# Short convolution with tokens on partitions, its shifts by DMA, and the first two output units interleaved, in a two-layer hybrid decoder trunk

## The reference

```
u = x * (1.0 + sc1) + sh1
proj = u @ w_in[l]                                   # 2048 -> 6144
q, k, v, gate_b, gate_c, h_in = split(proj)          # 1024 columns each
attn = dilated_mixture(rotary(q), rotary(k), v)      # 8 heads of 128
conv = gate_b * causal_short_conv(gate_c * h_in, conv_w[l])   # three taps: t-2, t-1, t
mixed = group_rms_norm(concat([attn, conv]), mix_norm_g[l])   # over groups of 128 columns
x = layer_norm(alpha * x + (1.0 + g1) * (mixed @ w_out[l]), ln1_g[l], ln1_b[l])
```

## Time and profile before

| | |
|---|---|
| timed runs | 2361.34, 2363.52, 2365.28 us |
| profiled execution, own time | 2359.68 us |
| its span | 2358.0 us |
| PE busy | 2275.1 us |
| DVE busy | 1727.1 us |
| ACT busy | 1101.9 us |
| moved by DMA | 623.15 MB, 264 GB/s in the mean |

### The profile page before, as it was taken

One profiled execution on the slowest core, in us unless ns is written; L12 is line 12 of the kernel. 1 busy time (PEld: TensorE's weight loads), 2 busy tenths in 40 slices (PEclk: granted clock), 3 DMA queues, 4 the chain that ended last, 5 costly groups with the idle time before them and its releaser, 6 DMA issues.

```text
span 2358.0 us, 30332 instructions
## 1 busy us (share of the span) xinstructions
PE 2275.1 (96%) x10480; PEld 1884.4 (80%) x10480; DVE 1727.1 (73%) x1929; ACT 1101.9 (47%) x1392; POOL 227.3 (10%) x400
## 2 busy tenths in 40 slices
PE   3899999999999999999999999999999999999997
PEld 2777887878888888888878888877888888888886
DVE  6889888877777777668878878777666555555566
ACT  1345543366445445435454554435553543543542
POOL 3311111110001001001010001101000000000000
PEclk9899999999999999999999999999999999999999
DMA  9987888967888888888966888886677776666574
GB/s 379 409 318 274 311 320 313 341 216 255 286 297 287 285 285 300 288 276 289 323 228 196 271 265 288 285 273 224 194 238 239 226 231 212 215 205 195 170 232 133
DMA packets 174734, 623.15 MB, mean 264 GB/s; under 512 B 19728, under 2 KB 20496, under 8 KB 174096
## 3 DMA queue, kind: packets, MB, share of 16 engines
q1 hardware_dynamic: 114128, 407.50, 50.6%
q0 software_dynamic: 55296, 201.35, 25.6%
q10 hardware_dynamic: 5184, 12.59, 1.7%
HBM read 619.27 MB, written 2.10 MB: 264 GB/s over the span
## 4 chain that ended last, share of the span: by engine, by line
PE 87%; DVE 6%; DMA 3%; issue 2%; ACT 1%; ACTq 0%; POOL 0%; DVEq 0%; SPq 0%; POOLq 0%
PE bank L1323 27%; PE bank L1325 26%; PE bank L1324 26%; DMA Z<-w_mod_dram 2%; DVE mod_acc L808 2%; PE bank L1428 2%; DVE w_lo L793 1%; PE bank L1337 1%; PE bank L1403 1%; PE bank L1339 1%; PE bank L1338 1%; ACT w_hi L480 1%; PE bank L1412 1%; DMA raw<-w_out_dram 0%; PE bank L1572 0%
## 5 line engine op out<-in xcount | busy, mean ns | idle before, releaser
L480 ACT ACTIVATE w_hi<-raw 128x1024 fp32r<-128x1024 f32 x764 | 807.6, 1059 | 1135.7 <-PE bank L1325 1015.2
L793 DVE TENSOR_TENSOR w_lo<-raw,w_hi 128x1024 fp32r<-128x1024 f32 x764 | 932.9, 1224 | 550.7 <-ACT w_hi L480 548.9
L1323 PE MATMUL bank<-w_hi,u_hi 128*128 128x512 f32 x1744 | 698.0, 400 | 0.3 <-DVE u_lo L851 0.3
L1325 PE MATMUL bank<-w_lo,u_hi 128*128 128x512 f32 x1744 | 684.1, 392 | 0.0
L1324 PE MATMUL bank<-w_hi,u_lo 128*128 128x512 f32 x1744 | 684.0, 392 | 0.0
L1323 PE MATMUL bank<-w_hi,m_hi 128*128 128x512 f32 x1200 | 470.9, 392 | 4.5 <-DVE m_lo L851 2.6
L1324 PE MATMUL bank<-w_hi,m_lo 128*128 128x512 f32 x1200 | 468.4, 390 | 0.0
L1325 PE MATMUL bank<-w_lo,m_hi 128*128 128x512 f32 x1200 | 468.3, 390 | 0.0
L1325 PEld LDWEIGHTS bank<-w_lo,u_hi 128*128 128x128 f32 x1744 | 330.5, 189 | 70.7
L1323 PEld LDWEIGHTS bank<-w_hi,u_hi 128*128 128x128 f32 x1744 | 330.9, 190 | 68.8 <-issue 1.4
L1324 PEld LDWEIGHTS bank<-w_hi,u_lo 128*128 128x128 f32 x1744 | 331.0, 190 | 68.0 <-issue 1.4
(11 more groups left out here) (144 smaller groups left out, 1138.3 us busy)
## 6 DMA issues: line engine op xcount, KB each, us to landing
raw<-w_ff_dram SPq DMA_DIRECT2D x512, 512.0 KB, 4.2
mod_raw<-w_mod_dram POOLq DMA_DIRECT2D x320, 512.0 KB, 5.6
raw<-w_in_dram SPq DMA_DIRECT2D x192, 512.0 KB, 5.3
Z<-w_mod_dram POOLq DMA_DIRECT2D x64, 512.0 KB, 11.0
raw<-w_out_dram SPq DMA_DIRECT2D x64, 512.0 KB, 6.1
gate<-b_rows_dram ACTq DMA_DIRECT2D x4, 1024.0 KB, 5.0
Z<-ln_g_dram ACTq DMA_DIRECT2D x16, 256.0 KB, 6.5
Z<-ln_b_dram ACTq DMA_DIRECT2D x16, 256.0 KB, 7.3
```

The costliest lines, as they stand in the source:

```text
L480: nc.scalar.activation(weights(w_hi, u_hi, unit, j), raw[:, j % RAW, :], ACT.Copy).then_inc(hi_ready, 1)
L793: nc.vector.tensor_tensor(weights(w_lo, u_lo, unit, j), raw[:, j % RAW, :], weights(w_hi, u_hi, unit, j).bitcast(F32), ALU.subtract).then_ ...
L1323: nc.tensor.matmul(o, hi[:, k, tok], wh, start=(k == 0), stop=False)
L1325: ins = nc.tensor.matmul(o, hi[:, k, tok], wl, start=False, stop=(k == KC - 1))
```

## The change

The convolution keeps tokens on partitions. A shift by one or two tokens is then a shift by partitions, done by DMA from A into `back[1]` (the tile B) and `back[2]` (the tile V): for a shift of one, 112 and 15 partitions and one row from the first half of the tokens to the second; for a shift of two, 126 partitions and two rows. ACT issues these five transfers at group 64 (88), after three loads that put the taps as rows on all partitions at 61 (72). DVE multiplies and adds in tiles of 128 x 1024 at groups 66 and 68 (90 and 92). B is no longer copied or transposed: DVE multiplies it in from its accumulator behind unit 8 + 3g. ACT sums squares with its accumulator at 72 (96), DVE scales by the root at 74 (98), and PE transposes once, at 77 (101), where ACT puts the gain in.

Units 12 and 13 are interleaved: j = 0 to 5 of unit 12, 0 to 5 of unit 13, then 6 and 7 of each; w_out is laid out in memory in that order. Their residuals run behind groups 109 and 111.

```diff
-Z_AT = [66, 90]
-B_AT = [72, 96]
-SSQ_AT = [74, 98]
-R_AT = [76, 100]
+ROWS_AT = [61, 72]
+SHIFT_AT = [64, 88]
+CONV_AT = [66, 90]
+SHIFT_ROWS = {1: ((0, 112), (112, 127)), 2: ((0, 126),)}
+SUM_AT = [72, 96]
+VAR_AT = [73, 97]
+ROOT_AT = [74, 98]
+Y_AT = [77, 101]
+def out_order(i):
+    if i < 12:
+        return i // 6, i % 6
+    return (i - 12) // 2, 6 + i % 2
+OUT_DONE = [max(i for i in range(2 * GROUPS) if out_order(i)[0] == u) for u in range(2)]
 # ACT
+            def load_taps(layer, g):
+                for tap in range(3):
+                    row = 3 * layer + tap
+                    act.dma_start(taps[:, tap, :], conv_rows[row:row + 1, g * NCOL:(g + 1) * NCOL]
+                                  .to_broadcast([P, NCOL])).then_inc(taps_in, 16)
+                        if p == SHIFT_AT[g]:
+                            act.wait_ge(acc_read[h_unit % 2], h_unit // 2 + 1)
+                            for d in (1, 2):
+                                for lo, hi in SHIFT_ROWS[d]:
+                                    act.dma_start(back[d][lo + d:hi + d, :, :], A[lo:hi, :, :]).then_inc(shift_in, 16)
+                                act.dma_start(back[d][0:d, 1, :], A[P - d:P, 0, :]).then_inc(shift_in, 16)
+                        if p == SUM_AT[g]:
+                            act.wait_ge(acc_read[b_unit % 2], b_unit // 2 + 1)
+                            for t in range(T):
+                                for h in range(4):
+                                    ins = nc.scalar.activation(squares[:, 4 * t + h, :], Y[:, t, h * P:(h + 1) * P],
+                                                               ACT.Square, accum_out=ssq[:, 4 * t + h:4 * t + h + 1])
+                            ins.then_inc(sum_ready, 1)
+                        if p == VAR_AT[g]:
+                            deviation(8 * layer + 2 + g)
+                        if p == Y_AT[g]:
+                            ...  # split with the gain, then split_high
 # DVE
+                        if p == CONV_AT[g] + 2:
+                            sync(nc.vector.tensor_tensor(A, A, taps[:, 2:3, :].to_broadcast([P, T, NCOL]), ALU.mult))
+                            sync(nc.vector.tensor_tensor(Y, Y, A, ALU.add))
+                        if p == 8 * (3 * g + 8) + 7:
+                            dve.wait_ge(pair_used, 8 * (base + u + 1))
+                            for t in range(T):
+                                ins = nc.vector.tensor_tensor(Y[:, t, :], pacc[u % 2][t][:], Y[:, t, :], ALU.mult)
+                            ins.then_inc(acc_read[u % 2], 1)
+                        if p == VAR_AT[g]:
+                            dve.wait_ge(sum_ready, 2 * layer + g + 1)
+                            nc.vector.tensor_scalar(ve[:], ssq[:], 1.0 / P, RMS_EPS, ALU.mult,
+                        if p == ROOT_AT[g]:
+                            sync(root(8 * layer + 2 + g, slice(0, 8)))
+                            nc.vector.tensor_tensor(y8, y8, rst[:].rearrange("p (i o) -> p i o", o=1).to_broadcast([P, 8, P]),
+                                                    ALU.mult).then_inc(y_ready, 1)
-                    if j == 7 and U_IN <= u < U_MIX - 1:
-                        residual(base + u, u % 2, u - U_IN, ALPHA)
+                    for i in range(2):
+                        if p == 8 * U_IN + OUT_DONE[i]:
+                            residual(base + U_IN + i, (U_IN + i) % 2, i, ALPHA, MIXER_AT[layer] + p + 1)
+                def convolve(layer, g):
+                    dve.wait_ge(taps_in, 48 * n)
+                    dve.wait_ge(shift_in, 16 * SHIFTS * n)
+                    nc.vector.tensor_tensor(Y, back[2], row(0), ALU.mult)
+                    sync(nc.vector.tensor_tensor(back[1], back[1], row(1), ALU.mult))
+                    sync(nc.vector.tensor_tensor(Y, Y, back[1], ALU.add))
 # PE
+            def out_units(layer, unit, side):
+                for i in range(2 * GROUPS):
+                    u, j = out_order(i)
+                    if j == 0:
+                        pe.wait_ge(acc_read[(unit + u) % 2], (unit + u) // 2)
+                    pe.wait_ge(split_ready, SPLITS * layer + 8 + j + 1)
+                    group(8 * unit + i, i % AHEAD, GK * j, pacc[(unit + u) % 2], m_hi, m_lo)
+                    side(i)
+                        if p == Y_AT[g]:
+                            pe.wait_ge(y_ready, 2 * layer + g + 1)
+                            for i in range(2):
+                                turn(JOB[("y", layer, g)] + i,
+                                     lambda c, t: Y[:, t, (2 * i + c) * P:(2 * i + c + 1) * P])
```

More of the change, by code:

```diff
@@ L99 @@
 O_AT = [[43, 59], [35, 59]]
-Z_AT = [66, 90]
-B_AT = [72, 96]
-SSQ_AT = [74, 98]
-R_AT = [76, 100]
+ROWS_AT = [61, 72]
+SHIFT_AT = [64, 88]
+CONV_AT = [66, 90]
+SHIFT_ROWS = {1: ((0, 112), (112, 127)), 2: ((0, 126),)}
+SHIFTS = sum(len(rows) + 1 for rows in SHIFT_ROWS.values())
+SUM_AT = [72, 96]
+VAR_AT = [73, 97]
+ROOT_AT = [74, 98]
+Y_AT = [77, 101]
 TAKEN = set()
@@ L199, in transpose_jobs, with build @@
     return at
-def build(nc, x, cond_c, ln_cols, w_in, w_out, w_ff1, w_ff2, w_mod, b_mod, b_rows, conv_w, mix_g, ln1_g, ln1_b,
+def build(nc, x, cond_c, ln_cols, w_in, w_out, w_ff1, w_ff2, w_mod, b_mod, b_rows, conv_rows, mix_g, ln1_g, ln1_b,
           ln2_g, ln2_b, cos, sin, mask, ident, out):
@@ L242, in build @@
         KT = Z[:, 5120:6144].rearrange("p (h n) -> p h n", h=4)
-        Y = KT
-        ZT = Z[:, 6144:7176].rearrange("p (h n) -> p h n", h=4)
+        Y = Z[:, 5120:6144].rearrange("p (t n) -> p t n", t=T)
+        back = [None, B, V]
+        squares = Z[:, 0:1024].rearrange("p (i n) -> p i n", n=P)
+        taps = Z[:, 6144:7680].rearrange("p (a n) -> p a n", a=3)
         QT = Z[:, 6144:7168].rearrange("p (h n) -> p h n", h=4)
@@ L320, in build @@
         sd_ready = sem("sd_ready")
-        sq_ready = sem("sq_ready")
-        rms_ready = sem("rms_ready")
+        taps_in = sem("taps_in")
+        shift_in = sem("shift_in")
+        sum_ready = sem("sum_ready")
+        y_ready = sem("y_ready")
         start_ready = sem("start_ready")
@@ L685, in side @@
[L685 to L704, removed]
-                                                     ACT.Copy).then_inc(split_hi, 1)
+                        if p == ROWS_AT[g]:
+                            if g:
+                                b_unit = base + 8
+                                act.wait_ge(acc_read[b_unit % 2], b_unit // 2 + 1)
+                            load_taps(layer, g)
@@ L1038, in start_quarter, with residual @@
                     one(5)
-            def residual(unit, par, s, alpha):
-                dve.wait_ge(pair_used, 8 * unit + 8)
+            def residual(unit, par, s, alpha, done):
+                dve.wait_ge(pair_used, done)
                 sl = slice(s * NCOL, (s + 1) * NCOL)
@@ L1136, in side @@
                             dve.wait_ge(t_read[job % 2], job // 2 + 1)
[L1137 to L1138 removed]
+                    for i in range(2):
+                        if p == 8 * U_IN + OUT_DONE[i]:
+                            residual(base + U_IN + i, (U_IN + i) % 2, i, ALPHA, MIXER_AT[layer] + p + 1)
+                    if j == 7 and U_IN + 2 <= u < U_MIX - 1:
+                        residual(base + u, u % 2, u - U_IN, ALPHA, MIXER_AT[layer] + p + 1)
                 def rotate(p, u):
@@ L1536, in side @@
                                     pe.wait_ge(o_read, head)
-                                if layer and head == 8 * layer:
-                                    pe.wait_ge(rms_ready, 2 * layer)
                                 col = slice(h * P, (h + 1) * P)
@@ L1668 @@
     w_in[:len(start)] = w_in[[GROUPS * unit + j for unit, j in start]]
+    w_out = _groups(np.asarray(w_out))
+    first = [out_order(i) for i in range(2 * GROUPS)]
+    for layer in range(DEPTH):
+        rows = w_out[U_OUT * GROUPS * layer:U_OUT * GROUPS * (layer + 1)]
+        rows[:len(first)] = rows[[GROUPS * unit + j for unit, j in first]]
     wm = w_mod.reshape(DEPTH, KC, P, 12 * D // 2 // SLAB, SLAB).transpose(0, 3, 1, 2, 4)
@@ L1674 @@
         "w_in": w_in,
-        "w_out": _groups(np.asarray(w_out)),
+        "w_out": w_out,
         "w_ff1": _groups(np.asarray(w_ff1)),
```

124 lines of the change are left out of this document (33 added, 91 removed).

## The result

The changed kernel takes 2374.07 us (median of 5 runs, 2371.28 to 2379.39) against 2363.52 before: ratio 1.0055, 95% interval 1.0044 to 1.0066. By the medians it is 10.6 us slower; the interval says 10 to 16 us. The prediction was 2355 with a range up to 2367; rival 2 gave 2375 for shifts that land late. The profiled execution took 2371.28 us, its span is 2369.6.

What follows compares the result with a forecast made beforehand. TensorE (PE), busy 2275.1 of 2358.0 us, was taken as the bound. Gains of 27.4 us less 17.9 given back left 9.5, taken as 8.5: 2355 us against 2363.52, range 2340 to 2367 (likeliest case 2350 to 2359).

Steps and rivals of the forecast that it cites:

- rival 2: DVE's wait before the convolution (groups 66, 90): shifts land late, each us beyond 10.6 costs 1 us four times; 2375; chance 0.17.
- the landing: Shift transfers on ACT's queue: last big one lands 9 to 12 us after group 64, taken as just hidden.
- the ledger: Whole kernel: 27.4 us gained by less PE work and fewer waits, 17.9 given back by new waits and lower clock.
- The terms for y: PE's transposes of y, groups 77 and 101: 8.6 us of new waits, including issue of the shifts on ACT.
- The single engine for 126 partitions: Shift by two: if one engine served it, landing takes 20 us and more, kernel 40 us slower; within rival 2.
- Traffic taken as hidden: DMA queues: taps and shifts, 7 MB in all, 1% of the traffic, hidden except in the chain to y.
- the terms for the issue alone: ACT issuing the shifts delays its conversions: 1.6 us a place in layer 0, about 1.0 in layer 1.
- PE work removed: PE, four places: fewer transposes, no sums of squares or turning of roots; 4.44 us a place, 17.8 in all.
- the mark of 14 us: Sign: if PE's busy time falls by less than 14 us, the step on removed PE work is wrong.
- Accumulators: Unit 14 waits for unit 12's banks, held by a residual: 0.8 us in layer 0, 5.0 in layer 1.
- Lower clock: PE at its lower clock behind the two longest new waits: charged twice, 3.5 us (0 to 7).
- Small edits: First g's memsets, fewer small loads and row tables in DRAM put at 0; taps and shifts mostly hidden.

## Why the prediction was wrong, step by step

**The step that failed** is the landing: "The last big one is issued by 3.5 to 4.8; the median landing on ACT's queue is up to 7.3 us: landed at 9 to 12. I take them as just hidden." The last issue came at 4.6 us after the end of group 64 (295.45 for 290.9), as said, but it landed after 13.5 us, at 18, and after 8.2 to 11.1 at the other places.

Three errors are in it. First, its own figures don't make it hidden: 3.5 or 4.8 us and 7.3 are 10.8 and 12.1, both beyond the 10.6 at which DVE comes, and the lower end of 9 takes a landing faster than the median. Second, landings of before were carried over to a stretch that had no room: its DMA engines were full, and 1 MB was put on top. No median of before would have warned, not even that of this very stretch (5.3 us for w_in); its busy share would have. With the shifts the loads there took 12.6 us, 11.1 with shifts that nobody waits for, and 5.8 without them. Third, and smaller, the transfers were priced by bytes alone, while parts of a tile landed up to a microsecond or so later than the whole.

That the added copies are what made the landings late is shown by these runs; how the engines divide their time among the queues, and so why a copy takes just this long, isn't.

DVE's start at 10.6 was right within a microsecond (it was ready 11.3 after group 64). DVE waited over 2 us at three of the four places, the mark that I had set for rival 2. That rival had the place (DVE's wait at groups 66 and 90), the price (each us costs one, four times) and the result (2375), with a chance of 0.17: the chance was wrong, not the mechanism. It was 17.8 us of waits where that rival has 20, and 16.2 us of time by the run with the wait taken away; that its 2375 is met within 1 us is partly luck, since the rest of the ledger moved too (below).

**A sum that was added up wrong.** The terms for y, 1.5 + 3.9 + 2 x 1.6 + 2 x 1.0, make 10.6, not 8.6: layer 1's share of the issue was left out. With it 19.9 us are given back and 7.5 are the net, so the forecast would have been about 2357. The sign doesn't hang on it.

**How a transfer is served.** Copies of 96, 112 and 128 partitions landed after 8.8, 9.0 and 7.8 us, against their bytes. By the Trainium skill, DMA: Bandwidth & Descriptors, "How many engines (k)", all three would be served by 16 engines. That the smaller ones then land first would be my inference, not the page's, and these medians don't bear it out. The single engine for 126 partitions, which would have made the kernel 40 us slower, isn't seen: in place of a second 112 they added 2.3 us to DVE's waits (16.3 for 14.0).

**What DVE's wait touches.** I followed DVE's chain to w_lo and to y. I missed that the slab sum at 305 us, which PE starts three groups behind the convolution, needs the step queued behind it on DVE: the 10.6 us at L1439 are no term of mine. The run with the sum moved shows it as a place where the wait surfaces; and with the transfers there but not waited for, 3.6 us are left at it (5.6 at all slab sums).

**Traffic taken as hidden.** "1 MB of shifts: 7 MB in all, 1% of the traffic; hidden by a conversion that runs four groups ahead". With the wait gone, issue and traffic cost 6.9 us; the terms for the issue alone (1.6 and 1.0 a place) make 5.2, so the traffic itself is 1.7 by the medians, inside the noise. The issues take 4.2 us for five, where the layer norm rows took 3.6.

**PE work removed, 17.8 us.** Right: 17.1 in the run without shifts. The page after shows 9.4, since matmuls at the lower clock are longer (the mark of 14 us that I set holds only for a trace without more of them, which the text should have said). L1464, the old L1428, counts 384, as said.

**Everything without the transfers.** The ledger without their issue gives 27.4 - 5.4 - 0.8 - 5.0 - 3.5 = 12.7; the run gave 12.5. Its parts match less well: y 3.3 us for 5.4, the residual 4.5 for 5.8, and 1.8 at the slab sum that I had at nothing. The agreement of the sum is partly luck.

**New waits for y.** 8.6 us expected (10.6 by its own terms), 7.7 after, but elsewhere: 3.6 at group 101 (5 expected), none at group 77, which the stall at the slab sum covers, and 2.3 and 1.8 in layer 1, where I had about none. The convolution's three products took 3.6 us, as counted; a pair of squares 0.29 us for the 0.35 of the earlier trace rows.

**Accumulators.** Layer 0: 0.8 us, as said. Layer 1: 2.2 for 5.0. In the run of the interleaving alone it is 2.1. The bounds were 0 to 6; I took the later load of w_out from before at nearly its full lateness, and it wasn't so late once residual and loads had moved: the longest wait for w_out there is 3.4 us where the earlier trace rows have 6.9.

**Lower clock.** Charged twice, seen in layer 0 behind three stalls (around 310 to 323, 395 to 400 and 415 to 425 us) and once in layer 1 (1450 to 1460); those of before went with their waits, as said, and these came behind others. Around the first stall alone it is 1.7 us on the slab sum and 11 matmuls at 0.43 for 0.227, 2.2 us: 3.9, more than both charges together.

**Small edits.** The memsets, put at nothing, take 0.96 us on DVE in front of w_lo. DVE's timeline of after:

```profile
291.93 0.48 DVE L1131 MEMSET Z<- 1x512 f32 x1
292.47 0.48 DVE L1132 MEMSET Z<- 2x512 f32 x1
```

Here DVE waits for the shifts behind them in any case, so they cost nothing; with the shifts in time they would eat up 2.5 groups' worth of the 0.38 us that DVE has over in each.

## What to carry to other kernels

Before a transfer is called hidden, look at the share of the DMA engines in the very stretch where it lands. Where they are full, no landing of before prices it, neither the run's median nor the stretch's own: here loads landed after 5.3 us in full engines until 1 MB was added, and after 12.6 then. A transfer that an in-order engine waits for has the cost of everything queued behind the wait, so follow each of these instructions to PE, the rare ones (a sum, a step) too. If it may be late, put first the part of the work that doesn't need it and give each transfer its own wait: with slab sum and y moved back to match, that was worth 12.5 us here.

## What the runs showed of the hardware

- Copies of 96 and 112 partitions landed after 8.8 and 9.0 us in the median, those of all 128 after 7.8, though they move less (one profile each, 5 to 13 us from copy to copy). The cause was not found.
- Copies within SBUF and reads from HBM in the same shapes made DVE wait the same (17.8 and 16.9 us).
- In the 20 us from 290 to 310, with the DMA engines at a share of 0.95 or more through the first 15 of them in every case, the w_in loads landed after 5.3 us in the median before, 5.8 without the shifts, 11.1 with shifts that nobody waits for, and 12.6 after. So here a busy share near 1 didn't by itself make loads late; adding 1 MB to it did.
- Five copies within SBUF held ACT for 4.2 us, the same shapes read from HBM for 2.0.
- A memset of one partition takes 0.48 us for 512 elements: few partitions don't make it cheap (a product of that length on 128 partitions takes 0.69).
